# Linear attention inside a fused network: one masked scan for each direction, and PSUM banks dealt out anew

## The reference, cut to what matters

```python
def gla_chunked(q, k, v, log_a):
    ...
    cum = jnp.cumsum(la, axis=3)
    last = cum[:, :, :, -1:, :]
    q_dec = q * jnp.exp(cum)
    k_intra = k * jnp.exp(-cum)
    k_state = k * jnp.exp(last - cum)
    mask = jnp.tril(jnp.ones((c, c), dtype=bool))
    scores = jnp.where(mask, jnp.einsum('nbhid,nbhjd->nbhij', q_dec, k_intra), 0.0)
    o_intra = jnp.einsum('nbhij,nbhjv->nbhiv', scores, v)

    def step(state, xs):
        qd, ks, vc, lst = xs
        o = jnp.einsum('bhid,bhdv->bhiv', qd, state)
        state = state * jnp.exp(lst[:, :, 0, :])[..., None] + jnp.einsum('bhjd,bhjv->bhdv', ks, vc)
        return state, o
```

## Time and profile before

| what | us |
|---|---|
| median of 3 runs | 3936.67 |
| lowest and highest | 3934.14, 3939.48 |
| the profiled execution | 3938.62 |
| its span (first to last instruction) | 3936.8 |
| PE busy | 3727.2 (95%) |
| DVE busy | 1827.7 (46%) |
| ACT busy | 842.1 (21%) |
| GpSimd busy | 2269.6 (58%) |

### The profile page before, as it was taken

How to read it: one execution, slowest core, us unless ns; L and a number is a source line. 1 busy time by engine, 2 the same in 40 slices (tenths; PEclk the granted TensorE clock), 3 DMA queues, 4 the chain that set the end, 5 groups by cost and what they waited for, 6 DMA issues and landing times.

```text
span 3936.8 us, 53124 instructions
## 1 busy us (share of the span) xinstructions
PE 3727.2 (95%) x21300; PEld 3017.7 (77%) x21300; DVE 1827.7 (46%) x2494; ACT 842.1 (21%) x1318; POOL 2269.6 (58%) x2218
## 2 busy tenths in 40 slices
PE   5999999999999899999899999999998999999997
PEld 4777678887777678887777677888787776778886
DVE  5644653244754652125543554523465435453325
ACT  3321110005121110003321532000243225220002
POOL 4523767785523677774446356777644453567773
PEclk9999999999999999998999999999989999999998
DMA  4223445342223443332223132333322331333332
GB/s 184 83 79 107 140 144 145 118 145 73 71 79 103 142 145 109 97 97 67 65 73 121 52 99 83 97 97 97 96 62 62 95 95 57 105 83 97 97 98 65
DMA packets 192196, 386.09 MB, mean 98 GB/s; under 512 B 21456, under 2 KB 21584, under 8 KB 190288
## 3 DMA queue, kind: packets, MB, share of 16 engines
q1 hardware_dynamic: 169776, 338.24, 29.1%
q10 hardware_dynamic: 22176, 44.45, 3.2%
HBM read 361.64 MB, written 20.97 MB: 97 GB/s over the span
## 4 chain that ended last, share of the span: by engine, by line
PE 83%; DVE 10%; ACT 4%; DMA 1%; issue 1%; ACTq 0%; SPq 0%; DVEq 0%
PE psum L415 17%; PE psum L417 17%; PE psum L416 17%; PE psum L487 3%; PE psum L489 2%; PE psum L488 2%; PE psum L509 2%; PE psum L970 1%; DVE units L1849 1%; PE psum L945 1%; PE psum L603 1%; PE psum L462 1%; PE psum L593 1%; PE psum L807 1%; PE psum L809 1%
## 5 line engine op out<-in xcount | busy, mean ns | idle before, releaser
L2249 POOL TENSOR_SCALAR w_hi<-raw 128x512 fp32r<-128x512 f32 x1082 | 747.0, 690 | 1523.4 <-DMA raw<-weight_chunks 1520.5
L2251 POOL TENSOR_TENSOR w_lo<-raw,w_hi 128x512 fp32r<-128x512 f32 x1082 | 1486.7, 1374 | 90.2
L415 PE MATMUL psum<-in_hi,w_hi 128*128 128x512 f32 x1920 | 761.7, 397 | 2.9 <-ACT mg L1545 1.3
L416 PE MATMUL psum<-in_lo,w_hi 128*128 128x512 f32 x1920 | 749.3, 390 | 0.0
L417 PE MATMUL psum<-in_hi,w_lo 128*128 128x512 f32 x1920 | 749.2, 390 | 0.0
L415 PEld LDWEIGHTS psum<-in_hi,w_hi 128*128 128x128 f32 x1920 | 361.9, 188 | 90.1 <-issue 11.1
L416 PEld LDWEIGHTS psum<-in_lo,w_hi 128*128 128x128 f32 x1920 | 361.8, 188 | 80.3 <-issue 6.2
L417 PEld LDWEIGHTS psum<-in_hi,w_lo 128*128 128x128 f32 x1920 | 361.5, 188 | 76.1
L487 PE MATMUL psum<-in_hi,w_hi 128*128 128x512 f32 x576 | 255.6, 444 | 20.0 <-ACT nt L1108 10.0
L488 PE MATMUL psum<-in_lo,w_hi 128*128 128x512 f32 x576 | 227.2, 394 | 0.0
L489 PE MATMUL psum<-in_hi,w_lo 128*128 128x512 f32 x576 | 227.0, 394 | 0.0
(11 more groups left out here) (430 smaller groups left out, 6703.7 us busy)
## 6 DMA issues: line engine op xcount, KB each, us to landing
raw<-weight_chunks SPq DMA_DIRECT2D x1082, 256.0 KB, 2.6
ada_col<-ada_slabs SPq DMA_DIRECT2D x80, 512.0 KB, 4.1
spill<-gate_st ACTq DMA_DIRECT2D x56, 256.0 KB, 2.8
ada_at<-ada_slabs SPq DMA_DIRECT2D x8, 1024.0 KB, 15.8
gin<-spill ACTq DMA_DIRECT2D x32, 256.0 KB, 3.2
mgs<-spill ACTq DMA_DIRECT2D x32, 256.0 KB, 2.9
sml<-small ACTq DMA_DIRECT2D x4, 1024.0 KB, 5.6
spill<-nt ACTq DMA_DIRECT2D x16, 256.0 KB, 2.6
```

What stands on the lines that cost most here:

```text
L415: pe.matmul(bank[:], wh, hi[:, i, :], start=(i == 0), stop=False)
L416: pe.matmul(bank[:], wh, lo[:, i, :], start=False, stop=False)
L2249: ts(w_hi[:, slot, :], raw[:, slot, :], 1.0, 1.0, ALU.mult, ALU.mult).then_inc(sem("chunk_hi"), 1)
L2251: ins = tt(w_lo[:, slot, :], raw[:, slot, :], w_hi[:, slot, :].bitcast(F32), ALU.subtract)
```

## The change

In the running sums, the scan goes over all 512 tokens at once, in place in `la`, with a mask `keep2` (2 KB in SBUF, filled by two memsets at the start of `block2`). The exclusive sum of the second direction is no longer made by a subtraction; the middle is subtracted while the sum is read one token to the left, and the first token of each chunk gets the negative middle by itself. The copies of the middle and of the last sum and the memsets of `dsc`'s last column are gone; ACT's exponential of `dsc` goes over three columns.

For PE, the side products of both attentions alternate between banks 2 and 3 (`bg2`), and the projections of these stages between banks 0 and 1 (`lin2`). The output projections (`p2a`, `p2b`) go back to `lin`, banks 0 to 2. The first core runs 8 side blocks ahead of its wait in place of 2.

```diff
+FILL_CORE = (8, 2, 2, 8)
...
-        used = {"lin": 0, "bg": 0, "aux": 0}
+        used = {pool: 0 for pool in ("lin", "bg", "aux", "lin2", "bg2")}
...
-        BANKS = {"lin": (0, 3), "bg": (3, 1), "aux": (4, 4)}
+        BANKS = {"lin": (0, 1, 2), "bg": (3,), "aux": (4, 5, 6, 7), "lin2": (0, 1), "bg2": (2, 3)}
+        uses_of = {}
...
-                n = used[pool]
-                first, banks = BANKS[pool]
-                b, uses = first + n % banks, n // banks
+                b = BANKS[pool][used[pool] % len(BANKS[pool])]
+                uses = uses_of.get(b, 0)
+                uses_of[b] = uses + 1
...
-                bank = begin(name, "lin")
+                bank = begin(name, lane[0], "lin")
...
-                fill((2, 2, 2, 8)[h])
+                fill(FILL_CORE[h])
...
-                side_jobs([(("g2a", l, m), "w_in2", l, N_GA + m) for m in range(DT)], "bg")
+                side_jobs([(("g2a", l, m), "w_in2", l, N_GA + m) for m in range(DT)], "bg2")
+                lane[0] = "lin2"
...
                 fill(DT * DT)
+                lane[0] = "lin"
                 for m in range(DT):
                     projection(("p2a", l, m), "w_o_gla", l, m, lambda i: ("split_ready", ("go", l, i)),
...
-                    for c in range(NCH):
-                        dve.tensor_tensor_scan(ln[h][i][:, c, :], kst[:, K_ONES, :], la[i][:, c, :], 0.0,
-                                                  ALU.mult, ALU.add).then_inc(sem("vector_step"), 1)
...
+                    ins = dve.tensor_tensor_scan(flat, keep2[:], flat, 0.0, ALU.mult, ALU.add)
...
+                    at = HB - 1 - i
+                    ins = tt(ln[h][i][:, :, i:P], la[i][:, :, 0:P - i],
+                             la[i][:, :, at:at + 1].to_broadcast([P, NCH, P - i]), ALU.subtract)
...
+                        ts(ln[h][1][:, :, 0], la[1][:, :, at], -1.0, None, ALU.mult).then_inc(sem("vector_step"), 1)
...
+                        ins = tt(dsc[h][1][:, 0:n], la[1][:, 0:n, P - 1], la[1][:, 0:n, at], ALU.subtract)
...
+                        ins = tt(dsc[h][1][:, 0:n], dsc[h][1][:, 0:n], la[1][:, 1:NCH, at], ALU.add)
                     else:
...
+                        ins = tt(dsc[h][0][:, 0:n], ln[h][0][:, 0:n, P - 1], la[0][:, 1:NCH, at], ALU.add)
...
+                for part, value in ((keep2[:], 1.0), (by_chunk(keep2[:])[:, :, 0:1], 0.0)):
+                    dve.memset(part, value).then_inc(sem("vector_step"), 1)
```

More of the change, by code:

```diff
@@ L225, in emit @@
         rope_t = ar("rope_t", 0, [P, 2, T])
+        keep2 = ar("keep2", 2, [P, T])
         go_hi = ar("go_hi", 4, [P, DT, T], F32R)
@@ L243, in emit @@
         ot = ar("ot", 90, [P, T])
-        mid = [ar(f"mid{i}", 94 + i / 32, [P, NCH]) for i in range(2)]
         dsc = [[ar(f"dsc{h}{i}", 94.0625 + (2 * h + i) / 32, [P, NCH]) for i in range(2)] for h in range(GH)]
@@ L802, in token_major @@
                     ts_ = slice(t * P, (t + 1) * P)
-                    bank = begin(name + (t,), "lin")
+                    bank = begin(name + (t,), lane[0], "lin")
                     for k in range(DT):
@@ L928, in block2 @@
                                hi=go_hi, lo=go_lo)
-                side_jobs([(("g2b", l, m), "w_in2", l, N_GB + m) for m in range(DT)], "bg")
+                side_jobs([(("g2b", l, m), "w_in2", l, N_GB + m) for m in range(DT)], "bg2")
+                lane[0] = "lin2"
                 for i in range(KVH):
@@ L1376, in gla_factors @@
                     act.wait_ge(sem("scalar_step"), passed("scalar_step"))
-                    af(dsc[h][i][:], dsc[h][i][:], ACT.Exp, scale=1.0 / TAU).then_inc(sem("ed_ready"), 1)
+                    af(dsc[h][i][:, 0:NCH - 1], dsc[h][i][:, 0:NCH - 1], ACT.Exp, scale=1.0 / TAU).then_inc(sem("ed_ready"), 1)
                     act.wait_ge(sem("ed_ready"), passed("ed_ready", (l, h, i)))
@@ L1957, in gla_decay @@
+                    ins.then_inc(sem("vector_step"), 1)
+                    dve.wait_ge(sem("vector_step"), passed("vector_step"))
+                    at = HB - 1 - i
+                    ins = tt(ln[h][i][:, :, i:P], la[i][:, :, 0:P - i],
+                             la[i][:, :, at:at + 1].to_broadcast([P, NCH, P - i]), ALU.subtract)
+                    ins.then_inc(sem("vector_step"), 1)
                     dve.wait_ge(sem("vector_step"), passed("vector_step"))
                     if i:
-                        tt(dsc[h][1][:, 0:n], dsc[h][1][:, 0:n], mid[1][:, 1:NCH], ALU.add).then_inc(sem("vector_step"), 1)
+                        ts(ln[h][1][:, :, 0], la[1][:, :, at], -1.0, None, ALU.mult).then_inc(sem("vector_step"), 1)
@@ L1966, in gla_decay @@
[L1966 to L1974, removed]
-                    else:
-                        dve.memset(dsc[h][1][:, n:NCH], 0.0).then_inc(sem("cum_ready"), 1)
-                        dve.wait_ge(sem("cum_ready"), passed("cum_ready", (l, h, i)))
+                        ins = tt(dsc[h][1][:, 0:n], dsc[h][1][:, 0:n], la[1][:, 1:NCH, at], ALU.add)
+                    else:
+                        ins = tt(dsc[h][0][:, 0:n], ln[h][0][:, 0:n, P - 1], la[0][:, 1:NCH, at], ALU.add)
@@ L1979, in gla_keys @@
+                    ins.then_inc(sem("cum_ready"), 1)
+                    dve.wait_ge(sem("cum_ready"), passed("cum_ready", (l, h, i)))
             def gla_keys(l, h):
```

15 lines of the change are left out of this document (4 added, 11 removed).

## The result

| | median us | lowest and highest |
|---|---|---|
| before, beside it | 3937.32 | 3934.14, 3939.48 |
| after | 3914.70 | 3907.27, 3920.86 |

The ratio is 0.995, with a 95% interval of 0.9937 to 0.9963: 0.5% faster, 20 us by the ratio and 22.6 by the two medians. The forecast was 3901.5 (35 us), its range 3887 to 3915. The sign and most terms were right. The median lies just inside the range; by the ratio, 0.995 of the 3936.67 that the forecast started from is 3917, just outside. More than a third of the gain is missing. The profiled execution took 3916.3 us, its span 3914.4, against 3936.8 before.

What follows compares the result with a forecast made beforehand. PE's idle waits on others bound the kernel, the longest 15.5 us a layer before L845. The terms -17.4 - 9.2 - 15.8 + 6.4 + 0.8 = -35.2 us gave 3901.5, range 3887 to 3915.

Steps and rivals of the forecast that it cites:

- The decay work on the path: DVE's running sums of head 3, linear attention: shrink from 15.7 to 11.1 us, 4.6 less.
- The 6.0 us between are exponentials on ACT and four products on DVE, which the change leaves alone: Between head 3's decay work and the matmul behind it: 6.0 us stay, so the wait falls as the work shrinks.
- Six side blocks ahead: fill(8) for fill(2) before L845: 18 more matmuls take 4.1 us off the 15.5 us wait.
- the bound of 12.7: Decay work of head 3 with every instruction at its GpSimd-disturbed length: 12.7 us, so only 3.0 less.
- In head 3 nothing is won: Second side-product bank, linear attention: no gain in head 3, where L876 follows the last state; waits only change name.
- list of signs: Profile signs: waits before `pt` or L876 replacing those removed would show the forecast wrong.
- Heads 1 and 2: Second side-product bank, linear attention: two bank waits there cost 1.2 us each, taken a little less.
- Ahead of `p2a`, attention, values, first key projection: Bank waits gone before the output projection and in attention (15.8 gained); two-bank projections lose 6.4 (values) and 0.8 (key).
- GpSimd doesn't disturb: Rival: decay work falls to 6.2 us, the wait to 1.9, low clock behind it goes; 3887, chance 0.08.
- The next reader is late: Rival: PE, arriving earlier, waits for softmax, state or split; second bank's gains (25) handed back; 3926.5, chance 0.13.
- The scan isn't shorter: Rival: a 512-column scan costs as much as four scans with pauses; 4.6 a layer go; 3911, chance 0.08.
- The new pauses cost clock: Rival: four pauses of 1.6 us among short matmuls lower the clock, 13.7 us each; 3956.5, chance 0.03.

Runs made afterwards that it cites:

- the first run: The kernel before with the new running sums alone (one masked scan, shifted read), old banks and fill(2): 3927.5 us, ratio 0.9982.

## Why the prediction was right and wrong, point by point

**The decay work on the path: right in its number.** Forecast 11.1 us, measured 11.3; alone, 4.5 us less. The way to it was sound: the mean of instructions beside GpSimd, plus a surcharge for long scans. The scans took 2.20 each, 0.98 above their 1.22.

**"The 6.0 us between are exponentials on ACT and four products on DVE, which the change leaves alone": the step that failed.** The change leaves their code alone, but not their neighbour. The six side blocks want two more weight chunks, GpSimd splits until 1909.3 in place of 1899.8, and the shorter sums bring the products into that time. It is 2.5 to 2.6 us a layer here, 5 to 5.4 in all. The prediction had seen GpSimd run on and put the effect into the sums only, where it was in the mean already.

**Six side blocks ahead: right for PE, wrong for the path.** They bring 4.1 us, and the fill ahead of `p2a` is shorter by that without a wait, as forecast; but DVE hands 2.6 of it back. The rule of the Trainium skill in "SBUF — State Buffer", section "SBUF: two separate sides" (a DVE instruction with two SBUF inputs and one of GpSimd that reads SBUF don't run side by side, the later one waits), was the warning, and I applied it to the sums alone. There the bound of 12.7 was too long against 11.3. On the products, which have two inputs each, the trace agrees with it: 1.64 and 1.63 for 0.69, and back to 0.69 in the run in which GpSimd is held. The copy of 1.10 us, which I had called agreement, reads one input only and is no instance of the rule as I told it.

**"In head 3 nothing is won", the waits "only change their name": wrong, since there was something to lose.** 4.1 us are lost in both layers. A wait of 1.35 for the bank (in front) and one of 1.02 for `ot` (behind) became 0.43 and 3.27. I had taken the moment at which `ot` is there as given. It moved 1.2 us back in every run with the second bank and eight blocks there, because GpSimd's next split comes earlier and falls on DVE's instructions: the same neighbour as in the step above. That the split comes earlier because PE, without its bank wait, frees its weights earlier is my reading; no run shows it by itself. And PE's earlier arrival turns the pause in front into waiting behind. As one stretch it has a price in clock, which I had worked out for the 3.3 us of the attention and didn't look for here. My list of signs was one step off: it spoke of waits before L876, the outputs, and this one is before the scores.

**Heads 1 and 2: half the size.** 2.1 of 4.2. The banks alone gain 3.0 in heads 0 to 2; in the changed kernel head 0 behind the long wait gives back up to 0.7 in a layer. I had taken 1.1 us for one wait of 0.7, and head 1 of layer 0 shows a new wait of 0.32 on `gs`.

**Ahead of `p2a`, attention, values, first key projection: right.** The stretches give -12.2, -14.9, +6.7 and +1.2 against -13.2, -15.8, +6.4 and +0.8. The last head of layer 0's attention now runs its 24 matmuls from 2292.56 to 2298.42, in 5.9 us against 11.07 in the earlier trace rows, at full clock:

```profile
2292.50:2311.10 18.60, 18.60 (x83) 14.11 (x82) 7.78 (x19) 8.34 (x15) 5.76 (x6) 1.00 0.29 85
```

**The rivals.** "GpSimd doesn't disturb" was false, but its number was good for the kernel in which GpSimd is kept from it: a wait of 1.9 was named, and 1.90 was measured. Its time of 3887 was too low for that kernel (3894.3), where head 3 still loses, and its "a pause of that length leaves the clock alone" held in six of eight places. "The next reader is late" came true in one place, head 3, and there the gain wasn't only handed back, but turned into a loss, in part because the reader's data came later than before. "The scan isn't shorter" falls with the first run. "The new pauses cost clock" fell: no low clock follows the four waits of 1.42 to 1.44.

The sum: of 12.8 us missing, 5.4 are the second row (GpSimd on the products), 4.1 head 3 (2.5 of them GpSimd again), 2.1 heads 0 to 2, 1.0 the last fill, 0.9 the attention, 0.7 values and `p2a`; unchanged code gave 1.4 back. What stays open is that last term, how long the wait in head 3 would be by PE's earlier arrival alone, and why the code ahead of the linear attention ends up to 8 us apart between programs that share it.

## What to carry over

Work that fills a wait of PE has a second consumer: its weights, masks or copies keep another engine busy, and the chain that everybody waits for may be that engine's neighbour. So price a filler by what it does to the chain, not by its matmuls alone, and consider holding the helper back while the chain runs (one wait of GpSimd, 16.7 us in the stretches concerned). The same holds for a wait that is removed: PE runs ahead, the helper's next piece of work moves with it, and both can make a later wait longer. A wait of 3.27 us cost clock here, where two of 1.35 and 1.02 had cost none.

## What the runs showed of the hardware

GpSimd's weight split makes DVE's instructions on SBUF longer: 0.16 to as much as 1.14 us for 128x3, 0.69 to 1.64 for 128x512, 1.22 to 2.20 for a scan of 512. It isn't only those with two inputs: the copy of 128x4 went from 0.17 to 1.11, and the rounding `go_hi` of 128x512 from 0.43 to 0.72 and 1.40. A chain of fourteen went from 12.2 to 19.8 us with the exponentials between. Two forms were left alone. `ot<-psum`, which reads PSUM, took 0.75 in all 16 places of the changed kernel, also at 2069.99 with a split beside it, and the reciprocal of 128x512 took 3.35 in all 20. GpSimd pays as well: its 0.62 us became 1.53.

Of the clock: behind waits of 2.62 and 3.27 us it was 0.50 for 3.4 us (6.8 once); behind the four of 1.42 to 1.44 and one of 1.99 it stayed at 1.00. Behind the wait of 1.90 in the four kernels with GpSimd held and the new sums it stayed at 1.00 in six places and was 0.50 for 3.4 us in two.
